# A hidden-layer shuffle in a decoder trunk: sixteen SBUF-to-SBUF transfers replaced by one into scratch memory and four out of it

## The reference, cut to what matters

```python
def swiglu_ffn(h, w_in, w_out):
    g, u = jnp.split(h @ w_in, 2, axis=-1)
    return (jax.nn.silu(g) * u) @ w_out

for l in range(DEPTH):
    x = x + 0.5 * swiglu_ffn(rmsnorm(x, norm_ffn1[l]), ffn1_w_in[l], ffn1_w_out[l])
    ...   # mixers, cross-attention
    x = x + 0.5 * swiglu_ffn(rmsnorm(x, norm_ffn2[l]), ffn2_w_in[l], ffn2_w_out[l])
return rmsnorm(x, norm_final)
```

## Time and profile before

| | |
|---|---|
| Time, median of 3 runs | 1118.09 us (1118.0 to 1118.31) |
| Profiled execution, its own time | 1116.31 us |
| Its span | 1114.6 us |
| PE busy | 1101.6 us, 99% of the span |
| DVE, ACT, POOL busy | 705.2, 541.7, 371.5 us |
| Mean granted PE clock | 0.997 of full speed |
| DMA, mean | 192 GB/s |

### The profile page before, as it was taken

The page is one execution under the profiler, slowest core; times in us unless marked ns, Lnnn a source line. Parts: engine busy times, 40 slices in busy tenths (PEclk is TensorE's granted clock), DMA queues, the critical chain, the costliest instruction groups (busy, mean ns, idle before and its releaser), DMA issues.

```text
span 1114.6 us, 13351 instructions
## 1 busy us (share of the span) xinstructions
PE 1101.6 (99%) x4998; PEld 911.9 (82%) x4998; DVE 705.2 (63%) x811; ACT 541.7 (49%) x599; POOL 371.5 (33%) x727
## 2 busy tenths in 40 slices
PE   8999999999999999999999999999999999999996
PEld 7888888888888888888888888888888888888885
DVE  6666655799655655654565656468986557666552
ACT  6454534845554544443454535357464545444431
POOL 0686820000000056773017767000000002676610
PEclk9999999999999999999999999999999999999998
DMA  8977565644553477766567676556454436766561
GB/s 261 298 231 210 188 218 175 216 158 135 206 189 98 131 230 223 216 214 198 187 201 220 212 227 197 187 189 205 144 184 168 165 116 193 214 213 217 190 206 62
DMA packets 181792, 214.29 MB, mean 192 GB/s; under 512 B 18186, under 2 KB 137558, under 8 KB 181728
## 3 DMA queue, kind: packets, MB, share of 16 engines
q1 hardware_dynamic: 158112, 200.82, 55.8%
q0 software_dynamic: 22528, 11.58, 3.9%
q10 hardware_dynamic: 1088, 1.05, 0.3%
HBM read 200.79 MB, written 1.05 MB: 181 GB/s over the span
## 4 chain that ended last, share of the span: by engine, by line
PE 88%; issue 5%; ACT 2%; DVE 2%; DMA 1%; POOL 1%; DVEq 0%; SPq 0%; POOLq 0%; ACTq 0%
PE acc L1291 27%; PE acc L1293 27%; PE acc L1292 27%; PE turn L1189 3%; PE acc L1484 1%; PE acc L1459 1%; DMA w_raw<-in_ffn_w_in 1%; ACT w_hi L423 1%; DVE w_lo L751 1%; POOL kT L388 1%; DVE arena L955 1%; PE acc L1262 0%; PE acc L1386 0%; PE acc L1263 0%; PE acc L1273 0%
## 5 line engine op out<-in xcount | busy, mean ns | idle before, releaser
L751 DVE TENSOR_TENSOR w_lo<-w_raw,w_hi 128x2048 fp32r<-128x2048 f32 x191 | 428.0, 2246 | 231.4 <-ACT w_hi L423 231.2
L423 ACT CAST w_hi<-w_raw 128x2048 fp32r<-128x2048 f32 x191 | 357.2, 1871 | 128.7 <-PE acc L1293 114.8
L388 POOL DMA_DIRECT2D kT<-kT x704 | 344.2, 497 | 161.0 <-DVE kT L862 117.9
L1291 PE MATMUL acc<-w_hi,xT_hi 128*128 128x512 f32 x872 | 342.3, 393 | 0.0
L1293 PE MATMUL acc<-w_hi,xT_lo 128*128 128x512 f32 x872 | 339.7, 390 | 0.0
L1292 PE MATMUL acc<-w_lo,xT_hi 128*128 128x512 f32 x872 | 339.3, 389 | 0.0
L1291 PE MATMUL acc<-w_hi,hT_hi 128*128 128x512 f32 x608 | 240.7, 396 | 0.8 <-DVE hT_lo L940 0.8
L1293 PE MATMUL acc<-w_hi,hT_lo 128*128 128x512 f32 x608 | 237.1, 390 | 0.0
L1292 PE MATMUL acc<-w_lo,hT_hi 128*128 128x512 f32 x608 | 236.6, 389 | 0.0
L379 POOL TENSOR_TENSOR rstd<-var,mhalf 128x2 f32<-128x2 f32 x14 | 24.2, 1730 | 575.5 <-DVE var L788 428.1
L1293 PEld LDWEIGHTS acc<-w_hi,xT_lo 128*128 128x128 f32 x872 | 163.7, 188 | 34.6
(11 more groups left out here) (111 smaller groups left out, 500.8 us busy)
## 6 DMA issues: line engine op xcount, KB each, us to landing
w_raw<-in_ffn_w_in SPq DMA_DIRECT2D x174, 512.0 KB, 5.0
w_raw<-in_ffn_w_out SPq DMA_DIRECT2D x80, 512.0 KB, 4.4
w_raw<-in_mix_w_in SPq DMA_DIRECT2D x32, 512.0 KB, 4.5
w_raw<-in_xattn_wkv SPq DMA_DIRECT2D x32, 512.0 KB, 4.3
kT<-kT POOLq DMA_DIRECT2D x704, 16.0 KB, 3.4
w_raw<-in_mix_w_out SPq DMA_DIRECT2D x16, 512.0 KB, 4.1
w_raw<-in_xattn_wq SPq DMA_DIRECT2D x16, 512.0 KB, 4.6
w_raw<-in_xattn_wo SPq DMA_DIRECT2D x16, 512.0 KB, 4.1
```

Source lines behind the costliest of these rows:

```text
L388: pool.dma_start(hfeat[B * q:B * q + B, g % 2, a * RUN:(a + 1) * RUN], hblk[B * a:B * a + B, g % 2, q * RUN:(q + 1) * RUN]).then_inc(hfeat ...
L423: act.copy(w_hi[:, u % SLOTS, 0:n], w_raw[:, u % SLOTS, 0:n]).then_inc(w_split_hi, 1)
L751: dve.tensor_tensor(w_lo[:, u % SLOTS, 0:n], w_raw[:, u % SLOTS, 0:n], w_hi[:, u % SLOTS, 0:n].bitcast(F32), ALU.subtract).then_inc(w_spli ...
L1291: pe.matmul(o, hi, wh, start=(first and j == 0), stop=False)
```

## The change

For each shuffle the 16 transfers within SBUF give way to one DMA of the whole of `hblk` (128 rows of 2 KB) into a scratch tensor in device memory, a wait on POOL until it has landed, and four DMAs back, one for each destination band of 32 partitions, each of 128 runs of 512 bytes. All five are issued by POOL. The scratch tensor has two buffers, as `hblk` and `hfeat` have. The constant `SHUFFLES`, from which the consumers' waits on `hfeat_landed` are worked out, goes from 16 to 4. Nothing else differs.

```diff
+        scratch = nc.dram_tensor("hidden_scratch", [2, P, GN], F32, kind="Internal").ap()
...
+        scratch_written = [sem(f"scratch_written{i}") for i in range(2)]
...
-        NBLK, RUN, SHUFFLES = P // B, 2 * T * B, 16
+        NBLK, RUN, SHUFFLES = P // B, 2 * T * B, 4
...
                 pool.wait_ge(hblk_ready, g + 1)
                 if g >= 2:
                     pool.wait_ge(hT_ready, g)
-                for a in range(NBLK):
-                    for q in range(NBLK):
-                        pool.dma_start(hfeat[B * q:B * q + B, g % 2, a * RUN:(a + 1) * RUN],
-                                     hblk[B * a:B * a + B, g % 2, q * RUN:(q + 1) * RUN]).then_inc(hfeat_landed[g % 2], 16)
+                pool.dma_start(scratch[g % 2], hblk[:, g % 2, :]).then_inc(scratch_written[g % 2], 16)
+                pool.wait_ge(scratch_written[g % 2], 16 * (g // 2 + 1))
+                rows = scratch[g % 2].rearrange("(a f) (q r) -> q f a r", a=NBLK, q=NBLK)
+                for q in range(NBLK):
+                    pool.dma_start(hfeat[B * q:B * q + B, g % 2, :].rearrange("f (a r) -> f a r", a=NBLK),
+                                   rows[q]).then_inc(hfeat_landed[g % 2], 16)
```

## The result

The changed kernel takes 1121.31 us (median of 15 runs, 1117.7 to 1126.8), the kernel before, timed beside it, 1116.75 us (15 runs, 1115.59 to 1119.75). The ratio is 1.0035, with a 95% interval of 1.0025 to 1.0045: slower, by 4.6 us between the medians (3.9 by the ratio). The time lies inside the forecast's range of 1116.5 to 1136 us, but its likeliest case, no change, did not come; the chance given to slower was 0.27.

The account below looks back on a forecast made before the run. PE was taken as the bound. Removed issues 0, reads and write 0, first shuffle +0.2 us gave a span of 1114.8, 1116.5 us profiled; plus 1.78 to the median, 1118.3 us. Range 1116.5 to 1136 us.

Parts of the forecast that it names:

- likeliest case, no change: Whole kernel: time within 0.2% of before, spanning 1116.8 to 1120.3 us; chance 0.70.
- rival 2: Slow round trip: W of 6.2 us makes POOL's turn 11.5 us, 0.6 over the period; 1136 us, chance 0.10.
- PE is the bound, and only the cover counts: PE is busy 1101.6 of 1114.6 us, so only whether the new shuffle stays inside its cover matters.
- A latency of up to 17.2 us costs nothing: Usual shuffle, transpose to cast: 12.2 us now plus 5.0 us of slack before PE begins unit 7.
- The first shuffle: First shuffle of the run: slack shrinks from 2.0 us to about 0, adding 0.2 us.
- t: Time in which POOL issues one DMA of 128 runs; taken as 1.2 us, bounds 0.50 and 1.98.
- W: Time from the write's issue to its landing as POOL sees it; taken as 5.0 us, bounds 2.7 and 6.2.
- Latency: From a shuffle's transpose to ACT's cast: 14.3 us, 2.1 more than now; bounds 9.2 and 18.1.
- POOL's turn: POOL's time for one shuffle: 10.3 us against a period of 10.88, fitting by 0.6 us.
- Rival 1: POOL becomes the bound by issue time: t of 1.98 us makes a turn 13.4 us; 1219 us, chance 0.17.
- DMA engines: The added write raises the busy share from 0.71 to about 0.78; weights have room, so zero cost.
- Rival 3: Faster: freer POOL queue and earlier landing help PE; 1115 us if 3 us were found, chance 0.03.

Follow-up runs that it names:

- the unwaited write: Kernel before with its 16 transfers, plus the write to scratch memory issued ahead and waited for only together with them, no read-back; 1119.86 us, ratio 1.0028.
- other blocks new: Changed kernel's shuffle only in the last three blocks, the first block keeping the 16 transfers of before; 1120.75 us, run again 1119.92 us.
- four writes: Changed kernel with the write cut in four, each read issued when its own write has landed; 1117.79 us, ratio 1.0008.
- pause behind: Changed kernel with one idle POOL masking instruction behind the four reads of each shuffle; 1124.89 us, ratio 1.0066.
- both with two pauses: Changed kernel with two idle POOL instructions ahead of each write, 1129.79 us; the same with the casts moved behind the second weight unit, 1120.36 us.
- cast later, old: Kernel before with hidden_hi and hidden_lo of the chunk before moved behind the second weight unit; 1116.32 us, ratio 0.9990.

## Why the prediction was right, and where it was wrong

The time fell inside the range, and that was partly luck. The upper part of the range was there for rival 2, a turn of POOL over its period, and the changed kernel's turn of 8.7 us was under it. The 4.6 us came by another way, which the prediction did not have. Its base was high, too: the three runs of before had a median of 1118.09 us, fifteen have 1116.75. So 1118.3 us missed by 3.0, while the forecast change of +0.2 us missed by 4.4.

- *PE is the bound, and only the cover counts.* Right. The removed 11 issues of each shuffle gave nothing: POOL's busy time fell from 371.5 to 146.5 us without a gain.
- *"A latency of up to 17.2 us costs nothing."* This is the step that failed. It followed one landing forward to the next weight unit and PE, where the 5.0 us are right for a single late shuffle. It left out that DVE's transpose for the next but one shuffle stands behind the same landing, on the same queue. A latency that stays high comes back each two chunks, and the sustained limit is 13.4 to 13.7 us. The forecast of 14.3 us would have been over it. Measured, this path cost 3.6 and 4.3 us of waits for `w_lo` in two profiles, where the prediction had no term for it.
- *The first shuffle.* I forecast its slack to shrink from 2.0 us to about 0 and +0.2 us. This held. In the first profile its latency went from 13.1 to 14.9 us and did not stop PE; in the second it was 15.6, and PE waited 0.48 us for that unit, just the 2.5 us less the slack of 2.0. But it left nothing for the turns that followed, each 0.9 us too long.
- *t.* Taken at 1.2 us between bounds of 0.50 and 1.98; measured 0.55. The price is almost all per instruction.
- *W.* Taken at 5.0, measured 5.9 in the median and up to 8.0 over all five DMAs. At the last shuffle of the second block, with the DMA engines busy for 0.73 of the time against 0.91 at the write before, POOL waited 3.0 us behind a 0.56 us issue, so W was 3.6; that load is the reason is likely, not shown. Going by the rows was right, and my 5.0 was still too low. The prediction had also estimated 2.6 us from the Trainium skill's "DMA: Bandwidth & Descriptors" (section "Anatomy of one DMA"); with 3.6 us at that write and 5.9 in the median this trace does not agree. The 0.2 us for POOL's wake after the landing came from no row of before; the chain above has 0.28 there.
- *Latency* of 14.3 us forecast, 13.5, 13.3, 12.9 and 12.7 measured in the four blocks: the errors in t and W partly cancel.
- *POOL's turn* of 10.3 us forecast; 0.3 + 0.56 + 5.6 + 2.2 = 8.7 measured. It did not bind: POOL still waited for DVE ahead of 38 of the 44 writes. Rival 1 (1219 us) is refuted by t. Rival 2 named a slow round trip, and W was near its 6.2 us, but it counted the cost through POOL's rate: 1136 us, where 1121 came.
- *DMA engines.* Right in the share: forecast 0.78 in the second block, measured 0.77, and ACT's waits for weights stayed at 6.8 us in 4 pieces. Wrong in taking a share with room to mean that nothing is late: with the unwaited write, which adds traffic and one issue of 0.56 us, the even shuffles of the first block came 1.4 us later.
- *Rival 3*, faster: nothing for it, as forecast.

## What to carry to other kernels

A wait that an idle engine can afford once is a different thing from one that it meets in each turn. Before a hidden latency is called free, go round the loop: from the landing through all that the two in-order queues have behind it, back to the instruction that releases the next such transfer, and compare the sum with the time that the bound engine takes for as many steps. And where a late transfer costs time, first look at what is queued behind its consumer: moving two calls here was worth as much as the whole change cost.

## What the runs showed of the hardware that I had not expected

- A POOL-issued DMA of 128 runs takes POOL 0.55 us, one of 32 runs 0.50.
- A 256 KB write to device memory landed 5.9 us after its issue in the median, and after 3.6 at a write during which the DMA engines were less busy (0.73 of the time); in quarters of 64 KB each landed after 4.7.
- The masking instruction over 128 by 800 elements took POOL 0.85 us in the median where it stood ahead of the write and 1.15 behind the reads, and up to 2.9: with two ahead, the pair took 4.1 us at most even shuffles of the first block, the first of it 2.8 in the chain shown. I don't know why.
- Two builds had a longer end with nothing in it: 9.9 us in two profiles of one, 7.6 in the other, against 6.4 to 6.5 in all the rest. In the 9.9 us the DMA engines carry nothing for the last 3.9, against 0.6 to 1.1 in the kernel before. I don't know why.
- The start varies between executions. In the first profile of "other blocks new" PE stood 2.9 us for `xT_lo` and was then granted half its clock, 1.2 GHz; the windows show it, with 2.9 us lost in the first stage against the kernel before:

```profile
18.00:20.00 2.00, 1.11 (x3) 0.92 (x4) 1.86 (x3) 1.94 (x3) 0.00 (x0) 0.56 0.89 293
20.00:22.00 2.00, 2.00 (x6) 1.55 (x5) 2.00 (x2) 1.91 (x5) 0.00 (x0) 0.50 0.27 93
```

The half clock is there from 18 to 22 us in four more profiles (four writes, pause behind, and both with two pauses), each behind waits for `xT_lo` of 2.1 to 2.6 us. It is in neither profile of the changed kernel, where PE waited 2.2 and 2.4 us for `xT_lo`, nor in "cast later, old" with its 2.2.

Such a start can explain a part of the spread of the kernel before (1115.4 to 1120.2 us over all its runs), but only profiled executions show it.
